# Head projection of a hybrid block: squares dealt out per tile, a plain tile at its end, weight buffers shared with the index stage

## The reference, cut to what matters

```python
h = rmsnorm(x, g_norm_mix)
proj = h @ w_in                      # 1024 -> D_in, split below
(aq, ak, av, iq, ik, iw, mq, mk, mv, mo, mi, mf, ga, gm) = jnp.split(proj, points, axis=-1)
aq = partial_rope(rmsnorm(aq..., g_q_att), positions)      # 8 heads of 64
ak = partial_rope(rmsnorm(ak..., g_k_att), positions)      # 2 heads of 64
iq = partial_rope(iq..., positions); ik = partial_rope(ik, positions)   # 8 heads of 32, 1 of 32
# indexer, per block of 128 queries
rel = relu(einsum('bqhd,bsd->bqhs', qi_b, k_idx))
score = einsum('bqhs,bqh->bqs', rel, wi_b) * idx_scale     # masked by chunks, then top 256
...                                  # sparse attention, mLSTM, output, routed experts
```

## Time and profile before

| | |
|---|---|
| runs, us | 3451.57, 3448.9, 3448.4 (median 3448.9) |
| profiled execution, us | 3453.41 |
| its span, us | 3451.8 |
| mean granted TensorE clock | 0.946 |
| TensorE, VectorE, ScalarE busy, share of the span | 87%, 72%, 53% |
| chain that ended last, by line | PE e_pY L728 8%; DMA e_xg 8%; PE e_pG L710 6% (the experts' stage) |
| tail matmuls (L1558), three groups of 1024, busy us | 402.1, 401.1, 401.1 |

### The profile page before, as it was taken

The page is one execution under the profiler, slowest core; times in us unless marked ns, Lnnn a source line. Parts: engine busy times, 40 slices in busy tenths (PEclk is TensorE's granted clock), DMA queues, the critical chain, the costliest instruction groups (busy, mean ns, idle before and its releaser), DMA issues. The chain is left out here.

```text
span 3451.8 us, 45088 instructions
## 1 busy us (share of the span) xinstructions
PE 3007.7 (87%) x12983; PEld 2230.6 (65%) x12984; DVE 2482.7 (72%) x3906; ACT 1815.0 (53%) x2523; POOL 446.2 (13%) x587
## 2 busy tenths in 40 slices
PE   6998699799899968999899589996699999999980
PEld 5765578588688634554455377775577777777760
DVE  5577588789989866676653335443898989889874
ACT  5322467576678434443334223332577777777760
POOL 0211110100000042212111000000111111111113
PEclk9999899999999979999999789998799999999995
DMA  3222322222222274454422556543569779666868
GB/s 122 81 72 67 105 82 71 65 75 73 68 65 74 71 180 126 115 111 96 85 71 51 161 164 189 166 152 110 200 245 368 273 287 348 232 226 254 312 266 346
DMA packets 367695, 536.99 MB, mean 156 GB/s; under 512 B 35632, under 2 KB 201040, under 8 KB 367424
## 3 DMA queue, kind: packets, MB, share of 16 engines
q1 hardware_dynamic: 338288, 430.70, 39.9%
q0 software_dynamic: 26960, 96.13, 7.6%
q10 hardware_dynamic: 2304, 8.39, 0.6%
HBM read 510.18 MB, written 129.80 MB: 185 GB/s over the span
## 5 line engine op out<-in xcount | busy, mean ns | idle before, releaser
L906 DVE TENSOR_TENSOR e_w_lo<-e_raw,e_w_hi 128x1024 fp32r<-128x1024 f32 x386 | 446.9, 1219 | 3.0 <-ACT e_w_hi L768 3.0
L1558 PE MATMUL x_ps<-h_hi,x_w_hi 128*128 128x512 f32 (+1 forms) x1024 | 402.1, 393 | 0.0
L1558 PE MATMUL x_ps<-h_lo,x_w_hi 128*128 128x512 f32 (+1 forms) x1024 | 401.1, 392 | 0.0
L1558 PE MATMUL x_ps<-h_hi,x_w_lo 128*128 128x512 f32 (+1 forms) x1024 | 401.1, 392 | 0.0
L768 ACT CAST e_w_hi<-e_raw 128x1024 fp32r<-128x1024 f32 x386 | 376.9, 1053 | 5.0 <-PE e_pG L710 5.0
L1748 DVE TENSOR_SCALAR_CACHE_REDUCE x_relu<-x_score,x_cand 128x1024 uint8<-128x1024 f32 (+3 forms) x217 | 315.6, 1487 | 3.6
L1661 ACT ACTIVATE x_relu<-x_score,x_cand 128x896 int8<-128x896 f32 (+3 forms) x217 | 281.0, 1296 | 56.4 <-DVE x_cand L1755 56.2
L2316 DVE CUSTOM_DVE_ANT_0 t_junk<-t_L,t_mask 128x512 bf16<-128x512 f32 (+3 forms) x320 | 185.7, 607 | 166.7 <-PE t_L L2098 165.7
L2137 PE MATMUL t_O<-t_probT,t_v 128*65 128x512 f32 x544 | 289.4, 614 | 13.8 <-ACT t_probT L2288 12.5
L2288 ACT ACTIVATE t_probT<-t_ST 128x512 f32<-128x512 f32 x272 | 160.4, 593 | 261.5 <-PE t_ST L2129 260.9
L710 PE MATMUL e_pG<-e_w_hi,e_x_hi 128*128 128x512 f32 x768 | 246.8, 402 | 3.6 <-DVE e_x_lo L901 3.6
(11 more groups left out here) (404 smaller groups left out, 6204.7 us busy)
## 6 DMA issues: line engine op xcount, KB each, us to landing
e_raw<-in_w_exp_gate SPq DMA_DIRECT2D x392, 256.0 KB
e_raw<-in_w_exp_up SPq DMA_DIRECT2D x392, 256.0 KB
e_raw<-in_w_exp_down SPq DMA_DIRECT2D x192, 512.0 KB
projT<-x_out SPq DMA_DIRECT2D x124, 256.0 KB
slot_out<-e_y POOLq DMA_DIRECT2D x48, 512.0 KB, 6.1
o_gate<-projT SPq DMA_DIRECT2D x32, 512.0 KB
x_w_raw<-in_w_in SPq DMA_DIRECT2D x31, 512.0 KB
a_tables<-in_x SPq DMA_DIRECT2D x16, 512.0 KB, 4.8
```

Source lines behind the costliest of these rows:

```text
L906: nc.vector.tensor_tensor(w_lo[:, u, :], raw[:, u, :], w_hi[:, u, :].bitcast(F32), ALU.subtract).then_inc(gl, 1)
L1558: last = nc.tensor.matmul(ps[0:w, u % 4, :], wt[:, m % 2, kk, 0:w], ht[:, kk, q * 512:(q + 1) * 512], start=(kk == 0 and s == 0), stop=(kk ...
```

## The change

- **Norm.** `squares(q)` for four tiles becomes `square(t)` for one, with a square root after each second tile; ScalarE does squares 0 to 3 and weights(0), and from then on copies tile t and squares tile t+4. A small square root of `eps` before the first square loads ScalarE's table at the start. VectorE takes reciprocals two at a time. TensorE issues the two steps of a unit ahead of the transposes of a tile, not behind them.
- **Loads.** `gain` comes after two token tiles and `w_raw` after four; positions and head gains come after the eighth.
- **Angles.** VectorE's angle block stands behind the norm and so do ScalarE's two sines.
- **Plain tile.** `ORDER` ends with tile 9, whose four units (36 to 39, `PLAIN` on) are copied to `X` and stored, with no rotation. The tail has 31 tiles, 124 units.
- **Shared buffers.** `w_raw`, `w_hi` and `w_lo` are allocated around both stages; the head also loads and splits the first two tiles of the tail (`READY`), in steps 34 to 41.
- **Tail.** TensorE does 16 parts (`AT_ONCE`, two units) before it waits for the scores' loads; `due()` starts at 16, and the planner spreads the other 976 parts over its steps.

```diff
-ORDER = (6, 7, 8, 4, 0, 1, 2, 3, 5)
+ORDER = (6, 7, 8, 4, 0, 1, 2, 3, 5, 9)
+READY = 2
+IDX, KEY, ROPED, PLAIN = 8, 12, 32, 36
...
-            if IDX <= u < KEY:
+            if IDX <= u < KEY or PLAIN <= u < HUNITS:
+                tile = ORDER[u // NCH]
                 sp.wait_ge(x_ok, u + 1)
-                sp.dma_start(proj[8 * P:9 * P, cols(u % NCH)], X[:, u % 3, :]).then_inc(x_st[u % NCH], 16)
-            if u >= 3:
+                sp.dma_start(proj[tile * P:(tile + 1) * P, cols(u % NCH)], X[:, u % 3, :]).then_inc(x_st[u % NCH], 16)
+            if 3 <= u < PLAIN + 3:
                 store(u - 3)
-            if u % NCH == 2 and u // NCH + 2 < HEAD:
+            if u % NCH == 2 and u // NCH + 2 < HEAD + READY:
                 load(u // NCH + 2)
...
         for t in range(NT):
-            turned(t)
             if t >= 4:
                 unit(t // 4 - 1, 2 * (t % 4), 2 * (t % 4) + 2)
+            turned(t)
...
+        def square(t):
+            act.wait_ge(x_in[t % XT], 16 * (t // XT + 1))
...
+            nc.scalar.activation(junk, x_t[:, t % XT, :], ACT.Square, accum_out=ss[:, t:t + 1]).then_inc(sq_done, 1)
+            if t % 2:
+                act.wait_ge(sq_done, t + 1)
+                nc.scalar.activation(rt[:, t - 1:t + 1], ss[:, t - 1:t + 1], ACT.Sqrt, bias=eps[:, :], scale=1.0 / DM).then_inc(rt_done, 1)
...
+        act.wait_ge(eps_ok, 1)
+        nc.scalar.activation(rt[:, 0:1], eps[:, :], ACT.Sqrt).then_inc(table_ok, 1)
+        act.wait_ge(table_ok, 1)
+        for t in range(4):
+            square(t)
         weights(0)
-        squares(1)
-        turned(0)
+        for t in range(NT):
+            turned(t)
+            if t + 4 < NT:
+                square(t + 4)
+            if t in (8, 12):
+                take(t // 4 - 2)
+            if t == 10:
+                weights(1)
+        take(2)
         act.wait_ge(sin_arg, 1)
...
-            if u % NCH == 1 and 2 <= u // NCH + 1 < HEAD:
+            if u % NCH == 1 and 2 <= u // NCH + 1 < HEAD + READY:
                 weights(u // NCH + 1)
...
+AT_ONCE = 2 * KT
...
-        self.per = self.total() / (UNITS * KT)
+        self.per = self.total() / (UNITS * KT - AT_ONCE)
...
-        return min(UNITS * KT, int(self.us / self.per))
+        return min(UNITS * KT, AT_ONCE + int(self.us / self.per))
...
+            while done < AT_ONCE:
+                part(done)
+                done += 1
             pe.wait_ge(loads, 80)
             z(0)
             z(1)
```

More of the change, by code:

```diff
@@ L973, with project_head @@
 UNITS = TAIL * NCH
-IDX, KEY, ROPED = 8, 12, 32
-def project_head(pg, h_hi, h_lo):
+IDX, KEY, ROPED, PLAIN = 8, 12, 32, 36
+def project_head(pg, h_hi, h_lo, w_raw, w_hi, w_lo):
     nc, i = pg.nc, pg.i
@@ L1042, in load @@
         def load(m):
+            tile = ORDER[m] if m < HEAD else m
             sp.wait_ge(wl_ok, m)
-            sp.dma_start(w_raw[:, :, :], w_v[:, :, ORDER[m] * P:(ORDER[m] + 1) * P]).then_inc(w_in, 16)
+            sp.dma_start(w_raw[:, :, :], w_v[:, :, tile * P:(tile + 1) * P]).then_inc(w_in, 16)
         def store(u):
@@ L1068, in tokens @@
             sp.dma_start(x_t[:, t % XT, :], i["x"][t * P:(t + 1) * P, :]).then_inc(x_in[t % XT], 16)
-        for t in range(4):
+        for t in range(2):
+            tokens(t)
+        sp.dma_start(gain, i["g_norm_mix"].partition_broadcast(P)).then_inc(consts, 16)
+        for t in range(2, 4):
+            tokens(t)
+        sp.dma_start(w_raw[:, :, :], w_v[:, :, ORDER[0] * P:(ORDER[0] + 1) * P]).then_inc(w_in, 16)
+        for t in range(4, XT):
             tokens(t)
@@ L1074, in _ @@
             sp.dma_start(gains[b * AD:(b + 1) * AD, 1:2], i["g_k_att"].rearrange("(d o) -> d o", o=1)).then_inc(loads, 16)
-        sp.dma_start(gain, i["g_norm_mix"].partition_broadcast(P)).then_inc(consts, 16)
-        sp.dma_start(w_raw[:, :, :], w_v[:, :, ORDER[0] * P:(ORDER[0] + 1) * P]).then_inc(w_in, 16)
-        for t in range(4, XT):
-            tokens(t)
         load(1)
@@ L1189, in _ @@
                 tables(8)
-            for x in range(u - LAG + 1) if u == FILL else [u - LAG] if u > FILL else []:
+            for x in range(u - LAG + 1) if u == FILL else [u - LAG] if FILL < u < PLAIN + LAG else []:
                 prepare(x)
@@ L1265, in _ @@
         nc.scalar.activation(kh[:, :, :], ang[:, :, :], ACT.Sin, scale=0.5).then_inc(sin_ok, 1)
-        squares(2)
-        turned(1)
-        squares(3)
-        take(0)
-        turned(2)
-        weights(1)
-        take(1)
-        turned(3)
-        take(2)
         act.wait_ge(loads, 16 * 5)
@@ L1348, in turned @@
                 v.tensor_tensor(h_lo[:, ks, at], aux[:, h % 2, :].rearrange("p (k n) -> p k n", n=P), h_hi[:, ks, at].bitcast(F32), ALU.subtract).then_inc(lo_done, 1)
+        dve.wait_ge(consts, 16)
+        for t in range(NT):
+            if t % 2 == 0:
+                inverse_roots(t // 2)
+            scaled(t)
+            if t:
+                turned(t - 1)
+            if t == 2:
+                weights(0)
+            if t == 12:
+                weights(1)
+        turned(NT - 1)
         dve.wait_ge(loads, 16 * 5)
@@ L1365, in _ @@
         v.tensor_scalar(A, A, 3.1415925, -3.1415925, ALU.min, ALU.max).then_inc(sin_arg, 1)
-        dve.wait_ge(consts, 16)
-        for t in range(NT):
-            if t % 4 == 0:
-                squares(t // 4)
-            scaled(t)
-            if t == 0:
-                weights(0)
-            if t:
-                turned(t - 1)
-            if t == 12:
-                weights(1)
-        turned(NT - 1)
         dve.wait_ge(sin_ok, 2)
@@ L1382, in _ @@
             expand(a)
-        for u in range(ROPED + 3):
+        for u in range(HUNITS + 2):
             if u == FILL + 2:
@@ L1493, in store @@
                 sp.dma_start(proj[at:at + w, (u % NCH) * 512:(u % NCH + 1) * 512], out_t[0:w, u % 2, :]).then_inc(stored[u % 2], 16)
-            load(0)
             for k in range(4):
@@ L1497, in _ @@
             sp.dma_start(IW[:, :, :], pg.d["iw"]).then_inc(loads, 16)
-            load(1)
             for m in range(TAIL):
@@ L1552, in part @@
                 if kk == 0:
-                    if q == 0:
-                        pe.wait_ge(wl_ok, m + 1)
+                    if q == 0 and m >= READY:
+                        pe.wait_ge(wl_ok, m - READY + 1)
                     if u >= 4:
@@ L1692, in project @@
                     state[0] += 1
-            weights(0)
-            weights(1)
-            state[0] = 2
+            state[0] = READY
             dve.wait_ge(setup, 1)
@@ L2455, in build @@
         h_lo = c.enter_context(nc.sbuf_tensor("h_lo", [P, KT, SEQ], F32R))
-        project_head(pg, h_hi, h_lo)
-        tail_and_index(pg, h_hi, h_lo)
+        w_raw = c.enter_context(nc.sbuf_tensor("w_raw", [P, KT, P], F32))
+        w_hi = c.enter_context(nc.sbuf_tensor("w_hi", [P, 2, KT, P], F32R))
+        w_lo = c.enter_context(nc.sbuf_tensor("w_lo", [P, 2, KT, P], F32R))
+        project_head(pg, h_hi, h_lo, w_raw, w_hi, w_lo)
+        tail_and_index(pg, h_hi, h_lo, w_raw, w_hi, w_lo)
     attend_and_recur(pg)
```

62 lines of the change are left out of this document (23 added, 39 removed).

## The result

| | before | after |
|---|---|---|
| median of all runs, us | 3451.2 (6 runs, 3448.4 to 3457.28) | 3434.6 (6 runs, 3431.09 to 3439.29) |
| ratio | | 0.9948, 95% interval [0.9937, 0.996] |
| profiled execution / its span, us | 3453.41 / 3451.8 | 3435.65 / 3434.0 |
| mean granted clock | 0.946 | 0.948 |

The kernel is faster by 16.6 us in the medians and by 17.8 in the spans. 3427.7 was forecast with a range of 3412 to 3445: right side, inside the range, 6.9 us low. The same kernel measured again later gave 3438.84 (5 runs) against 3451.84, which is 13.0 us faster, ratio 0.996 [0.9947, 0.9973].

What follows compares the result with a forecast made beforehand. It took ScalarE's order to bound the norm and TensorE's projection to pace the index rounds. Terms -12.9 + 0.5 + 13.0 - 4.2 - 16.5 - 1.1 = -21.2 us led to 3427.7 us, range 3412 to 3445.

Steps and rivals of the forecast that it cites:

- Part 1: Norm in the head: earlier first copies and about 2.5 us a tile bring the tables' transposes to 72.1, -12.9 us.
- Part 2: ScalarE's table loads in the head: four become three, one now at the keys' first root, +0.5 us of 0 to 1.3.
- Part 3: Plain tile at the end of the head: four more units there, next stage starts at 367.2, +13.0 us.
- Part 4: Start of the index stage: 16 parts run first, first score after 14.6 us against 18.8, -4.2 us.
- Part 5: Index stage's rounds: 976 parts paced instead of 1024 cut VectorE's waits, -16.5 us, and one weight split fewer, -1.1.
- A: Rival: the index stage keeps its length and its waits only move; 16.5 us back, 3444.2 us; chance 14%.
- B: Rival: TensorE bounds the index stage everywhere, six units fewer give 32.6 us instead of 17.6; 3412.7 us; chance 9%.
- C: Rival: the norm's interleaved work runs in series, 5.9 us a tile; 3465.1 us, slower than before; chance 5%.
- D: Rival: TensorE never gets its full clock in the norm, some 25 us over eleven tiles, 3453 us; chance 4%.

Runs made afterwards that it cites:

- pe_order: The changed kernel with TensorE's old order in the norm, a tile's transposes ahead of the two steps of a unit; 3431.81 us, ratio 0.9939 (again: 3431.73).
- root_early: once10 with ScalarE's table for the roots loaded early, by one small square root of eps behind the two sines; 3428.84 us, ratio 0.9927.
- norm_only: The kernel before with only the changed norm and loads; no plain tile, shared buffers or 16 parts at once; 3440.79 us, ratio 0.997.
- tail_only: The kernel before with plain tile, shared buffers, two ready tiles and 16 parts at once, the norm as before; 3447.21 us, ratio 0.9994.
- no_plain: The changed kernel without the plain tile; two ready tiles and 16 parts at once stay, 1008 parts paced; 3439.44 us, ratio 0.9962.
- two_thirds: pe_order with one of three matmuls (h_lo by w_hi) left out of each part of the index stage; 3424.8 us, ratio 0.9914.
- once0: pe_order with no parts done before the scores' loads instead of 16, 992 parts paced; 3433.94 us, ratio 0.9947.
- once10: pe_order with 10 parts instead of 16 before the scores' loads, 982 parts paced; 3427.88 us, ratio 0.9929 (again: 3429.64).
- after_again: The changed kernel unchanged, measured again beside later variants on one chip; 3438.84 us, ratio 0.996.
- plain2: pe_order with a second plain tile (tile 10) at the end of the head, 120 units left in the index stage; 3442.98 us, ratio 0.9982.

## Why the prediction was right, and where its sizes were off

**Part 1, the norm: the term that was mis-sized.** -12.9 was forecast, -9.9 measured (-10.7 in the second run). The start was better than I had it: tile 5 at 29.86, not 31.0. The ten tiles from there took 31.6 us, not 27.5. In the second profile these two were 30.95 and 29.7, so part of the good start is chance and the slow tiles are not. In the prediction's words "from there on a tile costs ScalarE 2.5, VectorE 2.5, TensorE 2.4": true for most tiles, but at tiles 8 and 12 (and 4) a new unit begins, its first steps need the lower half of the tile just before, and the change puts these steps ahead of the next tile's transposes. TensorE waits 1.93 and 2.25 us, with the transposes behind the wait, and then ScalarE and VectorE wait for these. These waits were in the forecast at nothing. In this execution the clock also falls to 0.50 for the steps and the transposes both times; in the three others with this order only at tile 12. I had read this order in the diff and named it, and checked engine sums, not what each step needs. pe_order shows it: the same work with the transposes first takes 25.8 us for the ten tiles, in both of its profiles. From tile 15 to the tables it was 13.65 us (13.64 before), as forecast: the angles and both sines are hidden.

**Part 2, table loads.** +0.5 forecast; root_early shows 0.4 at the next stage. norm_only lost 1.9 us between the tables and the next stage, of which this explains 0.4; the rest was not settled. In the changed kernel it does not show: tail_only, which has no such load among its keys, is 0.55 us shorter there than the changed kernel, and the load explains 0.4 of that.

**Part 3, the seam.** +13.0, and with Part 2 +13.5 against +14.0 measured. The size was right, the make-up was not, so that it came out is in part luck. I had the four units and one split of a weight tile (1.22). Step by step, the runs give 1.9 from the kernel before to norm_only, 4.5 from there to no_plain (the ready tiles) and 7.5 from there to the changed kernel (the plain tile). What the forecast left out are the 3.0 us at the value stores, which stand behind a ready tile's load on SP's queue: ScalarE waited 5.81 us for such a store at 344.53.

**Part 4, the start.** -4.2 forecast, -4.9 measured. The plain tile kept TensorE at work until 353.8, and it started its parts at the full clock, but ran at half for 3 us all the same (window 359 to 362.4 at 0.52): 12.6 us from the stage's start to the scores' matmuls, where I had 12.9. The loads landed after 8.24 us, not 11.

**Part 5, the rounds.** -16.5 and -1.1 forecast, -13.8 measured from first score to mask store. VectorE's waits for counts did shrink, and by about what was forecast: x_miss waits went from 29.5 to 14.8 (13 forecast), the 5.63 at 990.64 went too, though I had kept it (with 1008 parts, in no_plain, one of 5.6 is still there), x_out waits from 58.1 to 31.7, the rounds shrank by 15.7; 1.9 of that came back outside the rounds, in scores, signs and marks, which I had not looked at. Of the 3.8 us missing, then, 1.9 are this and the other 1.9 are rounds that shrank by 15.7 instead of 17.6. The prediction's sentence "There the projection sets the pace" is not borne out. TensorE without a gap was no sign of it: two_thirds takes 224 us of its work out of the changed stage, which gives 1.9, and is then 16.3 of 825.87 us below the kernel before. How the stage answers to the number of parts that are paced through it, over all kernels:

| parts paced | kernels | first score to mask store, us |
|---|---|---|
| 1024 | before, norm_only | 825.87, 827.16 |
| 1008 | no_plain | 822.36 |
| 992 | once0 | 819.26 |
| 982 | once10, once10_again, root_early | 816.36, 816.32, 814.25 |
| 976 | after, after_again, pe_order, pe_order_again | 812.09, 812.57, 811.51, 812.40 |
| 976, norm as before | tail_only | 814.55 |
| 976, two matmuls each | two_thirds | 809.61 |
| 944 | plain2 | 806.39 |

48 parts fewer are 48 x 3 x 0.226 = 32.5 us of TensorE, and the stage gives 13.8, some 0.29 us for each part of 0.68. Each step is worth less: the same 32 parts, with 16 done at once, give 10.3 us from no_plain to the changed kernel and 5.1 from pe_order to plain2. plain2 lies below two_thirds; it also takes a tile's cast, split and four copies out of the stage. The same code of this stage varies by 0.5 to 3.0 us from profile to profile (982 and 976 parts, tail_only included), so single steps in the table are not finer than that.

**The rivals.** A (the stage keeps its length) fell: 13.8 us shorter. B (TensorE bounds it everywhere, -32.6) fell: 13.8, and two_thirds puts the floor at -16.3. C (norm in series) fell: 2.41 us a tile. D (half clock through the norm) came in small: in the profiled execution two falls of the clock of some 3 us, in three others with this order one, not eleven tiles. The kernel before has such a fall too (0.50 in 54 to 58, behind a wait of 3.89 us). The Trainium skill (TensorE: Matmul & The Clock Gate, "HAM oscillation") describes a kernel whose waits between groups of matmuls bring the clock down every time; its waits are longer. The traces agree with that in part: the wait of 2.24 or 2.25 us ahead of tile 12 was followed by half clock in all four executions, the one of 1.93 or 1.94 ahead of tile 8 in one of the four. Taking both waits out gave 5.8 us over the ten tiles in the first pair of profiles and 4.0 in the second, for 4.2 us of waits.

**Sum.** Of the 6.6 us by which the marks missed (-21.2 against -14.6), 3.0 are Part 1, 3.8 Part 5, 0.5 the seam, and Part 4 gave 0.7 back. The 3.2 us of later stages went the other way, by variation as far as can be told, and brought the total nearer to the forecast by luck.

## What to carry to other kernels

When work is dealt between the steps of a pipeline, check for each dealt piece which product of the step before it needs; where a new group begins, put the independent work (here the transposes) ahead of the dependent step, since an in-order queue turns one late operand into a stop for three engines, and here at times into a fall of the clock as well. Before moving work out of a stage that one engine seems to bound, take a third of that engine's work out once and see how far the time falls: here the floor was 16.3 us below, while 32.5 us of TensorE were moved. A busy share of 100% does not answer that question. Filler paid once here, where it lay beside stores and waits (7.5 us at the seam for 21.7 of work, 10.3 back in the stage behind); the second one cost its full 21.7 and gave 5.9 back. A version with the transposes first, 10 parts at the start and the early table load (root_early, 3428.84, or 0.9927 of the kernel before) is faster than both kernels; the last two of these three edits can't be told from pe_order alone by the medians.

## What the runs showed of the hardware that I had not expected

- The same short pause brings TensorE's clock down in one execution and not in the next. After TensorE had stood idle for 1.93 us (to 37.78), two matmuls went at or near the full clock, then the clock was at half (0.50 in 38.3 to 41.6), though the engine had no further pause. In the second profile, norm_only and no_plain the pause was 1.93 or 1.94 us too and the clock stayed at 1.00; the pause of 2.24 or 2.25 before tile 12 was followed by 0.50 in all four. Behind the seam the fall also came once work had resumed: the first matmuls of the stage at 358.28, after 4.47 us of waiting, were at full pace, those from 359.38 on lasted 0.63.
- The granted clock of the first 28 us can't be read off: its row says 1.00 for 20 to 28.4, and the matmuls from 25.02 to 26.73 start 0.43 us apart, as at half clock, where later ones start 0.23 apart.
- A table load of 1.28 us had its activation 1.30 us behind its own start (157.45 to 158.75), and behind the last sine it began with no pause (60.84 + 0.29 to 61.15). It cost the critical path 0.4 us.
- Two executions of one kernel differ by 3 us and more in stages behind the change (spans 3434.0 and 3437.3, mask stores 1184.19 and 1183.82), so a change of 5 us in a part of this kernel is told by its marks, not by its total. The marks vary too: tables by 0.8 us (75.12 and 74.32), the mask store of once10 by 1.4 (1178.92 and 1177.56).
